# A two-layer decoder trunk on one core: the program's begin by contraction halves, its end shared among three engines, extra identity transposes, and one slab rounded earlier

## The chip, the core and the metric

The kernel runs on one core of a Trainium2 chip. The metric is the device time in microseconds of one execution; a trace of one profiled execution of the kernel before is read beside it.

## The reference, cut to what matters

Six sub-layers in a row work on x, 512 tokens by 1024 features, float32. After each stands a LayerNorm.

```python
def swiglu(x, w1, w3, w2):
    return (jax.nn.silu(x @ w1) * (x @ w3)) @ w2
# DEPTH = 2, D_FF = 2816; w = 1/2 for the gated (SwiGLU) layers, 1 for the mixers
for l in range(DEPTH):
    x = layer_norm(ALPHA * x + 0.5 * swiglu(x, w1[l,0], w3[l,0], w2[l,0]), ...)
    h = hybrid_attention(x, ...) if l % 2 == 0 else hgrn2(x, ...)
    x = layer_norm(ALPHA * x + h, ...)
    x = layer_norm(ALPHA * x + 0.5 * swiglu(x, w1[l,1], w3[l,1], w2[l,1]), ...)
```

## The kernel before, in words

The program has six phases, called n = 0 to 5: gated layer, attention, gated layer, gated layer, HGRN, gated layer. Every large product is made of three passes in a rounded float32 format: each operand is split into a high part (a rounded copy) and a low part (the operand minus its high part), and TensorE adds high x high, high x low and low x high (`three`, L1388 to L1390).

**Weights.** They come in slabs of 128 x 2048 numbers, 1 MB each, into a ring of three buffers `raw`; SP issues the loads in order (`load_slab`, L514). ScalarE makes the high part of a whole slab (`high`, L726, into `w_hi`), GpSimd the low part in four quarters of 128 x 512 (`low`, L664, into `w_lo`); for the first two slabs of the program VectorE makes the low part instead (`first_low`, L1258). Semaphores `hi_ready` and `lo_ready` count slabs. A slab buffer can be rounded into again when TensorE has finished its last user.

**Activations.** x stays in SBUF as four tiles of 128 tokens. At a phase's begin TensorE turns each tile with eight identity transposes (L1409) into two PSUM banks, four contraction blocks of 128 features in each bank; ScalarE copies a bank as high part into `xt_hi` (L731), VectorE makes the low part in `xt_lo` (L950). `begin` on TensorE turns tiles 0 and 1, waits for the first slab and the low parts, runs the first products for the first 256 tokens (two blocks of outputs from the first slab, one from the second), turns tiles 2 and 3, and goes on. Where the phase before is a gated layer (n = 1, 3, 4), tiles 0 and 1 are turned inside that layer's last products instead.

**A gated layer** projects 256 columns at a time with w1 and w3 (`up`), and works the down projection two groups at a time by a scheme with seven products of half size (P1 to P7) instead of eight. For it VectorE makes sums of operands (`left_sum`, L973; `right_sum`, L989) and low parts (L979, L995), ScalarE high parts (L750, L759). The four pairs are p = 0 to 3. In pair 0, TensorE runs `up` of slab s0+4, P1, P2, then `up` of slab s0+5. ScalarE's order for pair 0 is: high parts of A12, S1, B11, then `high(s0 + 5)`, then S2, S3, S4, A22. Every engine works its own queue strictly in the written order, and waits on semaphores in it.

**The end of a phase** (`last_down_and_norm`): the last down projection gives eight pieces of 512 features, in order of tile and half. VectorE adds the two pieces of a tile to x (`add_piece`, L1051), takes moments (L1211 to L1215), GpSimd makes rstd (L671), and `normalise` is two VectorE operations of 128 x 1024 with a wait for rstd between: centre and multiply by the gain `lng` (L1222), then scale by rstd and add the bias `lnb` (L1226). In the last phase SP stores a tile when `ln_done` counts it (L611).

**The program's begin**, in the kernel before: SP loads x tile 0, slab 0, x tile 1, slab 1, x tiles 2 and 3, three small inputs. ScalarE's order is: turned tile 0, slab 0, turned tile 1, slab 1, turned tiles 2 and 3. VectorE follows the same order with the low parts.

Of the kernel before, what the change touches and what calls it, by code (L numbers as in the profile page):

```python
# [25 lines left out]
F32 = mybir.dt.float32  # L26
F32R = mybir.dt.float32r
ALU = mybir.AluOpType
# [172 lines left out]
def build_trunk(nc, x_in, w1, w3, w2, ln_g, ln_b, aw_in, sinks, aw_out, hw_in, hnorm, hw_out, lbs_in, out,  # L201
# [23 lines left out]
    with ExitStack() as ctx:  # L225
# [109 lines left out]


        x_loaded = [sem(f"x_loaded{t}") for t in range(NT)]
        ident_zeroed = sem("ident_zeroed")
        consts_ready = sem("consts_ready")
        raw_landed = [sem(f"raw_landed{i}") for i in range(RING)]  # L340
# [24 lines left out]
        var_ready = sem("var_ready")  # L365
        rstd_ready = sem("rstd_ready")
        centred = sem("centred")
        ln_done = sem("ln_done")
        turn_done = sem("turn_done")
        xt_hi_done = sem("xt_hi_done")  # L370
# [137 lines left out]
        def _(sp):  # L508
# [36 lines left out]
            def load_x(t):  # L545
                sp.dma_start(x[:, t, :], x_in[0, t * P:(t + 1) * P, :]).then_inc(x_loaded[t], 16)

            def load_small():
# [4 lines left out]
            load_x(0)  # L553
            for n, (kind, wi, _, _) in enumerate(phases):
                s0 = bases[n][0]
                if kind == "ffn":
                    l, f = wi
                    a, b, c = w1[l, f], w3[l, f], w2[l, f]
                    load_slab(s0, up_slab(a, 0))
                    if n == 0:  # L560
                        load_x(1)
                    load_slab(s0 + 1, up_slab(b, 0))
                    if n == 0:
                        load_x(2)
# [23 lines left out]
                else:  # L588
                    for s, (name, g) in enumerate(mixer_slabs(kind)):
                        if s == RING:  # L590
                            load_params(n)
                        if kind == "attn":
                            swa, moba = 8 * HD, 8 * HD + 4 * HD
                            col = {"q": g * GW if g < 2 else moba + (g - 2) * GW, "kv": swa,
                                   "kb": moba + 512 + (g - 2) * GW, "vb": moba + 1024 + (g - 2) * GW}
                            src = down_slab(aw_out[0], g) if name == "down" else \
                                aw_in[0][:, col[name]:col[name] + GW].rearrange("(c p) n -> p c n", p=P)
                        else:
                            src = down_slab(hw_out[0], g) if name == "down" else \
# [3 lines left out]
                        if n == 0 and s == 0:  # L603
                            load_x(1)
                        if n == 0 and s == 1:
                            load_x(2)
                            load_x(3)
                            load_small()
            for t in range(NT):
                sp.wait_ge(ln_done, NT * last_phase + t + 1)  # L610
                sp.dma_start(out[0, t * P:(t + 1) * P, :], x[:, t, :]).then_inc(out_stored, 16)  # L611
            sp.wait_ge(out_stored, 16 * NT)


        @block.gpsimd
        def _(pool):
# [55 lines left out]
                                       ALU.pow).then_inc(rstd_ready, 1)  # L672


            pool.wait_ge(lo_ready, 2)
            low(2)
            for n, (kind, _, _, _) in enumerate(phases):
                s0 = bases[n][0]
                if kind == "ffn":
# [3 lines left out]
                    for j, tiles in enumerate(((0, 1), (2, 3), ())):  # L683
                        if n < last_phase:
                            if j == 2:
                                pool.wait_ge(ln_done, NT * (n + 1))
                            low(s0 + FFN_RING + j)
                        norm_powers(n, tiles)
                else:
                    slabs, plan = mixer_slabs(kind), mixer_schedule(kind)  # L690
                    if kind == "attn":
# [29 lines left out]
        def _(act):  # L721
# [50 lines left out]
                turn_high(turn, 2)  # L772
                turn_high(turn, 3)

            turn_high(0, 0)
            high(0)
            turn_high(0, 1)
            high(1)
            turn_high(0, 2)
            turn_high(0, 3)  # L780
# [74 lines left out]
            for n, (kind, _, _, _) in enumerate(phases):  # L855
                s0, K0, H0 = bases[n]
                if kind == "ffn":
# [7 lines left out]
                    gates(G0 + 1)  # L865
                    right_high(n, fi, 0, "B21")
                    for p in range(NP):
                        left_high(fi, p, "A12")
                        left_high(fi, p, "S1")
                        right_high(n, fi, p, "B11")  # L870
                        high(s0 + 4 * p + 5)
                        for name in ("S2", "S3", "S4", "A22"):
                            left_high(fi, p, name)
                        gates(G0 + 2 * p + 2)
# [64 lines left out]
                                high(s0 + s)  # L939
                if n < last_phase:  # L940
                    turn_all_high(n + 1, bases[n + 1][0] + 2)


        @block.vector
        def _(dve):
# [257 lines left out]
            def last_down_and_norm(n, K, weight):  # L1203
# [28 lines left out]

                add_pieces(0)
# [25 lines left out]
            turn_low(0, 0)  # L1261
            first_low(0)
            turn_low(0, 1)
            first_low(1)
            turn_low(0, 2)
            turn_low(0, 3)
# [118 lines left out]
        def _(pe):  # L1385
# [6 lines left out]
            def features(out_, slot, j, tok):  # L1392

                for c in range(DC):
                    cols = slice(c * GW + j * P, c * GW + (j + 1) * P)
# [24 lines left out]
            def product(n, f, p, name, b0):  # L1420
# [7 lines left out]
                for t in range(2):  # L1428
# [6 lines left out]
                                   (b_hi_[:, c, :], b_lo_[:, c, :]), c == 0, c == 1)  # L1435
                    mm.then_inc(product_done, 1)

            def begin(n, first_two):

                K = bases[n][1]
                if n == 0 or phases[n - 1][0] != "ffn":
                    turn(n, 0)
                    turn(n, 1)
                pe.wait_ge(lo_ready, bases[n][0] + 1)
                if n:
                    pe.wait_ge(y_added, FREE_AT_START + 8 * K - 2)
                pe.wait_ge(xt_lo_done, 8 * n + 4)
# [101 lines left out]
            def ffn_first_two(s0):  # L1551
                def first_two(s, half, tiles):
                    tok = slice(half * T // 2, (half + 1) * T // 2)
                    for j in tiles:
                        mm = features(bank[2 * s + j][:, tok], slot_of[s0 + s], j, tok)
# [238 lines left out]
```

## Time and profile before

| what | value |
| --- | --- |
| median of 3 runs | 2015.11 us (2015.10 to 2016.25) |
| the profiled execution | 2015.4 us, its span 2013.7 us |
| TensorE products | busy 1970.4 us, 98% of the span |
| VectorE | 1064.2 us, 53% |
| GpSimd | 921.8 us, 46% |
| ScalarE | 629.7 us, 31% |
| mean granted TensorE clock | 0.993 of full |

The span goes from the first to the last instruction. PE is TensorE (PEld its weight loads), DVE VectorE, ACT ScalarE, POOL GpSimd, SP the engine that issues the loads (SPq its queue). L1388 is line 1388 of the kernel before. A busy engine can be blocked inside an instruction: the time then stands in that instruction's duration. Idle time of an engine that is not on the path to the end costs nothing.

### The profile page before, as it was taken

The page shows a single profiled execution, that of the slowest core. Times are in us where ns is not written, and L with a number is a line of the kernel's source. Part 1 is how long each engine was busy: PE and PEld are TensorE (multiplying, and loading weights), DVE is VectorE, ACT ScalarE, POOL GpSimd, SP SyncE. Part 2 cuts the span into 40 slices and gives each one's busy share as a digit, 9 for nine tenths or more (in the row PEclk, how much of TensorE's full clock was granted, in tenths as well). Part 3 has the DMA queues.
Part 4 walks back from the last instruction along what each step waited for, and adds up shares of the span by engine and source line. Part 5 has one row for each costly group of instructions (what it writes and reads, how often), then busy time and mean ns, then how long its engine had stood idle before and what let it go on. Part 6 is the DMA issues. An engine that isn't in the chain of part 4 may idle for free.

```text
span 2013.7 us, 25063 instructions
## 1 busy us (share of the span) xinstructions
PE 1970.4 (98%) x10329; PEld 1682.5 (84%) x10329; DVE 1064.2 (53%) x1467; ACT 629.7 (31%) x786; POOL 921.8 (46%) x598
## 2 busy tenths in 40 slices
PE   8999999999989999999999999999999999999997
PEld 7888888988879888888988888898998988888886
DVE  2555472554363665654466656353543674466545
ACT  3333232254332333322233332232232123233330
POOL 4554464632223655445456535543443344465533
PEclk9999999999999999999999999999999999999999
DMA  6232323221204233232423323241211203323221
GB/s 231 84 107 82 126 84 105 89 84 43 68 16 147 84 111 109 74 105 84 147 84 105 104 85 105 84 126 59 68 64 64 63 25 123 126 84 120 89 85 42
DMA packets 135137, 185.45 MB, mean 92 GB/s; under 512 B 3168, under 2 KB 119024, under 8 KB 135024
## 3 DMA queue, kind: packets, MB, share of 16 engines
q1 hardware_dynamic: 134864, 183.59, 27.4%
q8 instruction: 82, 1.34, 0.3%
q10 hardware_dynamic: 160, 0.26, 0.1%
q14 instruction: 31, 0.25, 0.0%
HBM read 181.48 MB, written 2.10 MB: 91 GB/s over the span
## 4 chain that ended last, share of the span: by engine, by line
PE 92%; DVE 4%; POOL 3%; ACT 1%; issue 0%; DMA 0%; SPq 0%; DVEq 0%; ACTq 0%
PE psum L1388 28%; PE psum L1389 28%; PE psum L1390 28%; PE psum L1651 3%; POOL w_lo L664 2%; PE psum L1627 1%; PE psum L1594 1%; PE psum L1409 1%; PE psum L1609 1%; DVE x L1051 0%; ACT w_hi L726 0%; DVE x L1222 0%; PE psum L1689 0%; PE psum L1679 0%; DMA raw<-in_ffn_w 0%
## 5 line engine op out<-in xcount | busy, mean ns | idle before, releaser
L664 POOL TENSOR_TENSOR w_lo<-raw,w_hi 128x512 fp32r<-128x512 f32 x524 | 867.0, 1686 | 929.2 <-ACT w_hi L726 904.6
L1388 PE MATMUL psum<-xt_hi,w_hi 128*128 128x512 f32 (+1 forms) x1824 | 680.0, 373 | 11.9 <-DVE xt_lo L950 7.4
L1389 PE MATMUL psum<-xt_lo,w_hi 128*128 128x512 f32 (+1 forms) x1824 | 674.9, 370 | 0.0
L1390 PE MATMUL psum<-xt_hi,w_lo 128*128 128x512 f32 (+1 forms) x1824 | 674.9, 370 | 0.0
L1388 PEld LDWEIGHTS psum<-xt_hi,w_hi 128*128 128x128 f32 x1824 | 347.6, 191 | 75.5 <-issue 12.1
L1390 PEld LDWEIGHTS psum<-xt_hi,w_lo 128*128 128x128 f32 x1824 | 347.2, 190 | 57.4
L1389 PEld LDWEIGHTS psum<-xt_lo,w_hi 128*128 128x128 f32 x1824 | 347.7, 191 | 55.4
L726 ACT ACTIVATE w_hi<-raw 128x2048 fp32r<-128x2048 f32 x133 | 253.7, 1910 | 304.9 <-PE psum L1390 304.0
L1011 DVE SCALAR_TENSOR_TENSOR x<-psum,x 128x512 f32<-128x512 f32 x224 | 146.0, 685 | 134.8 <-PE psum L1390 131.1
L740 ACT ACTIVATE gate<-psum 128x512 f32<-128x512 f32 x88 | 52.5, 597 | 310.1 <-PE psum L1390 310.0
L1388 PE MATMUL psum<-w_hi,h_hi 128*128 128x512 f32 x352 | 140.1, 398 | 2.6 <-DVE x L1051 2.6
L1051 DVE SCALAR_TENSOR_TENSOR x<-psum,x 128x512 f32<-128x512 f32 x128 | 85.9, 687 | 105.4 <-PE psum L1390 105.1
L1388 PE MATMUL psum<-w_hi,xt_hi 128*128 128x256 f32 (+2 forms) x448 | 140.5, 314 | 0.0
L1389 PE MATMUL psum<-w_lo,h_hi 128*128 128x512 f32 x352 | 138.6, 394 | 0.0
L1390 PE MATMUL psum<-w_hi,xt_lo 128*128 128x256 f32 (+2 forms) x448 | 137.6, 307 | 0.0
L1389 PE MATMUL psum<-w_lo,xt_hi 128*128 128x256 f32 (+2 forms) x448 | 137.5, 307 | 0.0
L1390 PE MATMUL psum<-w_hi,h_lo 128*128 128x512 f32 x352 | 137.3, 390 | 0.0
L1389 PE MATMUL psum<-w_lo,a_hi 128*128 128x512 f32 x320 | 126.2, 394 | 0.0
L1388 PE MATMUL psum<-w_hi,a_hi 128*128 128x512 f32 x320 | 125.5, 392 | 0.0
L958 DVE TENSOR_TENSOR hid<-psum,gate 128x512 f32<-128x512 f32 x48 | 33.2, 692 | 173.7 <-PE psum L1390 173.7
L1390 PE MATMUL psum<-w_hi,a_lo 128*128 128x512 f32 x320 | 124.3, 389 | 0.0
L995 DVE TENSOR_TENSOR w_lo<-raw_odd,w_hi 128x1024 fp32r<-128x1024 f32 x48 | 59.1, 1232 | 110.5 <-ACT w_hi L759 110.5
(153 smaller groups left out, 2206.9 us busy)
## 6 DMA issues: line engine op xcount, KB each, us to landing
raw<-in_ffn_w SPq DMA_DIRECT2D x116, 1024.0 KB, 5.4
raw_odd<-in_ffn_w SPq DMA_DIRECT2D x16, 1024.0 KB, 5.0
raw<-in_hgrn_w_in SPq DMA_DIRECT2D x16, 1024.0 KB, 5.4
raw<-in_attn_w_in SPq DMA_DIRECT2D x9, 1024.0 KB, 5.3
raw<-in_attn_w_out SPq DMA_DIRECT2D x4, 1024.0 KB, 4.9
raw<-in_hgrn_w_out SPq DMA_DIRECT2D x4, 1024.0 KB, 4.9
lng<-in_ln_g SPq DMA_DIRECT2D x6, 512.0 KB, 4.2
lnb<-in_ln_b SPq DMA_DIRECT2D x6, 512.0 KB, 5.3
```

The costliest lines, as they stand in the source:

```text
L664: op = pool.tensor_tensor(w_lo[:, slot_of[s], cols], raw[:, slot_of[s], cols], w_hi[:, slot_of[s], cols].bitcast(F32), ALU.subtract)
L726: act.activation(w_hi[:, slot_of[s], :], raw[:, slot_of[s], :], ACT.Copy).then_inc(hi_ready, 1)
L740: act.activation(gate[:, j, :], bank[j][:], ACT.Silu).then_inc(gate_done, 1)
L958: dve.tensor_tensor(dst[:, j, :], bank[2 + j][:], gate[:, j, :], ALU.mult).then_inc(hid_done, 1)
L995: dve.tensor_tensor(lo, right_source(n, name), hi.bitcast(F32), ALU.subtract).then_inc(right_lo_ready, 1)
L1011: dve.scalar_tensor_tensor(out=x_piece(row, t, half), in0=bank[b0 + t][:], scalar=weight / ALPHA, in1=x_piece(row, t, half), op0=ALU.mult, ...
L1051: dve.scalar_tensor_tensor(out=part, in0=banks[k % len(banks)][:], scalar=weight / ALPHA, in1=part, op0=ALU.mult, op1=ALU.add).then_inc(y_ ...
L1388: pe.matmul(out_, w[0], xs[0], start=first, stop=False)
L1389: pe.matmul(out_, w[0], xs[1], start=False, stop=False)
L1390: return pe.matmul(out_, w[1], xs[0], start=False, stop=last)
L1409: mm = pe.transpose(bank[4 + 2 * (t % 2) + b][:, c * P:(c + 1) * P], x[:, t, (4 * b + c) * P:(4 * b + c + 1) * P], ident[:])
L1651: mm = pe.matmul(out_, ks[:, g % 2, h, chunk], rhs, start=True, stop=True)
```

## The change

It has four parts.

1. The program's first phase begins by contraction halves. x tiles 0 and 1 are loaded in halves of 512 features, slab 0 in two halves of four contraction blocks each; the order of the loads is x half 0 of tiles 0 and 1, slab half 0, x half 1 of both tiles, slab half 1, slab 1, then as before. TensorE turns block 0 of both tiles, then block 1 of both; ScalarE and VectorE round block, slab half, block, slab half. The first product group (first slab, first output block, first 256 tokens) starts when the first half is ready and waits for the second half ahead of its fifth contraction block. Behind the transposes of block 0 stand twelve extra identity transposes, behind those of block 1 eight, written to a bank that nobody reads.
2. At the begins of n = 2 and n = 5 (behind the mixers) fourteen extra identity transposes stand between the wait for the added pieces and the wait for `xt_lo`.
3. In pair 0 of every gated layer ScalarE rounds slab s0+5 ahead of A12, S1 and B11 instead of behind them.
4. At the end of the last phase VectorE centres tiles 0 and 1, ScalarE scales them by rstd, GpSimd adds the bias. VectorE goes on to tiles 2 and 3 and waits for tiles 0 and 1 to be finished ahead of normalising tile 2. The last operation on tile 3 is cut in two halves of 512 features, and each half is stored by itself.

In the diff `sp`, `pool`, `act`, `dve` and `pe` are the queues of SP, GpSimd, ScalarE, VectorE and TensorE.

```diff
+            for t in range(2):
+                load_x_half(t, 0, x_half_loaded[t])
...
-                    load_slab(s0, up_slab(a, 0))
                     if n == 0:
-                        load_x(1)
+                        load_first_half(0, up_slab(a, 0), raw_half_landed)
+                        for t in range(2):
+                            load_x_half(t, 1, x_loaded[t])
+                        load_first_half(1, up_slab(a, 0), raw_landed[0])
+                    else:
+                        load_slab(s0, up_slab(a, 0))
                     load_slab(s0 + 1, up_slab(b, 0))
...
+            for half in range(2):
+                cols = slice(half * HALF, (half + 1) * HALF)
+                sp.wait_ge(ln_done, NT * last_phase + NT + half)
+                sp.dma_start(out[0, (NT - 1) * P:T, cols], x[:, NT - 1, cols]).then_inc(out_stored, 16)
...
+            def shift(n, tiles):
+                pool.wait_ge(par_loaded[1], 16 * (n + 1))
+                for t in tiles:
+                    pool.wait_ge(scaled, t + 1)
+                    pool.tensor_tensor(x[:, t, :], x[:, t, :], lnb[:], ALU.add).then_inc(ln_done, 1)
...
+            first_turn_high(0)
+            act.wait_ge(raw_half_landed, 16)
+            act.activation(w_hi[:, 0, 0:SLAB // 2], raw[:, 0, 0:SLAB // 2], ACT.Copy).then_inc(hi_half_ready, 1)
+            first_turn_high(1)
+            act.wait_ge(raw_landed[0], 16)
+            act.activation(w_hi[:, 0, SLAB // 2:SLAB], raw[:, 0, SLAB // 2:SLAB], ACT.Copy).then_inc(hi_ready, 1)
...
                     for p in range(NP):
+                        if p == 0:
+                            high(s0 + 5)
                         left_high(fi, p, "A12")
                         left_high(fi, p, "S1")
                         right_high(n, fi, p, "B11")
-                        high(s0 + 4 * p + 5)
+                        if p:
+                            high(s0 + 4 * p + 5)
...
+            for t in range(2):
+                act.wait_ge(centred, NT * last_phase + t + 1)
+                act.wait_ge(rstd_ready, NT * last_phase + t + 1)
+                act.activation(x[:, t, :], x[:, t, :], ACT.Copy, scale=rstd[:, t:t + 1]).then_inc(scaled, 1)
...
+                if n == last_phase:
+                    dve.wait_ge(par_loaded[0], 16 * (n + 1))
+                    centre(0)
+                    centre(1)
+                    add_pieces(2)
+                    moments(2)
+                    add_pieces(3)
+                    moments(3)
+                    dve.wait_ge(ln_done, NT * n + 2)
+                    normalise(2)
+                    centre(3)
+                    dve.wait_ge(centred, NT * n + 4)
+                    normalise_halves(3)
+                    return
...
+            def keep_clock(times):
+                for _ in range(times):
+                    pe.transpose(bank[1][:, 0:P], ident[:], ident[:])
...
+                if n == 0:
+                    for b in range(2):
+                        for t in range(2):
+                            pe.wait_ge((x_half_loaded, x_loaded)[b][t], 16)
+                            for c in range(4):
+                                mm = pe.transpose(bank[4 + 2 * t + b][:, c * P:(c + 1) * P],
+                                                  x[:, t, (4 * b + c) * P:(4 * b + c + 1) * P], ident[:])
+                            mm.then_inc(turn_done, 1)
+                        keep_clock((12, 8)[b])
+                    pe.wait_ge(lo_half_ready, 1)
+                    pe.wait_ge(xt_lo_done, 2)
+                else:
...
                     pe.wait_ge(y_added, FREE_AT_START + 8 * K - 2)
+                    if phases[n - 1][0] != "ffn":
+                        keep_clock(14)
+                    pe.wait_ge(xt_lo_done, 8 * n + 4)
```

## Rows read from the trace of the kernel before

**Rows 1.** Waits of TensorE: us in total, times, longest us.

```profile
PE psum L1388 <- DVE xt_lo L950: 7.4, 3, 2.6
PE psum L1388 <- POOL w_lo L664: 4.2, 4, 1.1
```

**Rows 2.** Timeline of the begin: start, length, engine, operation, [idle before <- what ended it].

```profile
4.72 1.94 PE L1409 MATMUL psum<-ident,x 128*128 128x128 f32 x8 [4.72 <-DMA x<-in_x]
...
5.85 0.60 ACT L731 ACTIVATE xt_hi<-psum 128x512 fp32r<-128x512 f32 x1 [3.76 <-PE psum L1409]
...
7.88 1.91 ACT L726 ACTIVATE w_hi<-raw 128x2048 fp32r<-128x2048 f32 x1 [0.59 <-DMA raw<-in_ffn_w]
...
9.30 1.97 PE L1409 MATMUL psum<-ident,x 128*128 128x128 f32 x8 [2.63 <-DMA x<-in_x]
...
12.28 1.91 ACT L726 ACTIVATE w_hi<-raw 128x2048 fp32r<-128x2048 f32 x1 [0.38 <-DMA raw<-in_ffn_w]
...
13.46 0.55 PE L1388 MATMUL psum<-xt_hi,w_hi 128*128 128x256 f32 x1 [2.20 <-DVE xt_lo L950]
...
14.22 2.29 DVE L1258 TENSOR_TENSOR w_lo<-raw,w_hi 128x2048 fp32r<-128x2048 f32 x1 [0.90 <-ACT w_hi L726]
...
24.03 1.91 PE L1409 MATMUL psum<-ident,x 128*128 128x128 f32 x16
```

**Rows 3.** Stretches: length, busy (count) of PE, PEld, DVE, ACT, POOL, PEclk, DMA, GB/s.

```profile
13.40:17.40 4.00, 3.94 (x18) 3.97 (x19) 2.29 (x1) 0.79 (x1) 0.00 (x0) 1.00 0.49 162
17.40:24.00 6.60, 6.60 (x56) 6.60 (x55) 0.00 (x0) 0.00 (x0) 0.00 (x0) 1.00 1.05 376
604.70:608.00 3.30, 3.30 (x18) 3.30 (x17) 3.23 (x8) 0.00 (x0) 1.53 (x2) 0.51 0.00 0
1646.80:1652.40 5.60, 5.57 (x26) 5.60 (x27) 5.43 (x12) 0.00 (x0) 3.08 (x4) 0.50 0.00 0
1382.50:1389.40 6.90, 6.90 (x25) 6.07 (x26) 2.56 (x5) 0.00 (x0) 2.32 (x2) 0.54 0.47 150
```

**Rows 4.** Timeline of TensorE behind the attention phase, and in the HGRN phase.

```profile
598.39 1.03 PE L1409 MATMUL psum<-ident,x 128*128 128x128 f32 x8
600.68 1.09 PE L1409 MATMUL psum<-ident,x 128*128 128x128 f32 x8 [1.25 <-DVE x L1226]
604.36 0.35 PE L1388 MATMUL psum<-xt_hi,w_hi 128*128 128x256 f32 x1 [2.59 <-DVE xt_lo L950]
...
1382.47 1.94 PE L1651 MATMUL psum<-arena 128*128 128x64 f32 x10 [2.14 <-DVE arena L1156]
```

**Rows 5.** Timeline of VectorE at the same begin.

```profile
601.74 2.48 DVE L950 TENSOR_TENSOR xt_lo<-psum,xt_hi 128x512 fp32r<-128x512 f32 x4
```

**Rows 6.** Timeline of the second slab of the first gated layer, all engines.

```profile
62.56 0.69 DVE L958 TENSOR_TENSOR hid_odd<-psum,gate 128x512 f32<-128x512 f32 x1 [4.75 <-PE psum L1390]
...
65.50 1.90 ACT L726 ACTIVATE w_hi<-raw 128x2048 fp32r<-128x2048 f32 x1
...
67.48 7.62 POOL L664 TENSOR_TENSOR w_lo<-raw,w_hi 128x512 fp32r<-128x512 f32 x1 [17.01 <-ACT w_hi L726]
...
72.73 1.22 DVE L989 TENSOR_TENSOR raw<-right_sums,raw 128x1024 f32<-128x1024 f32 x1
74.08 2.10 DVE L989 TENSOR_TENSOR raw_odd<-raw_odd,raw 128x1024 f32<-128x1024 f32 x1
...
78.57 1.27 POOL L664 TENSOR_TENSOR w_lo<-raw,w_hi 128x512 fp32r<-128x512 f32 x1
...
79.89 0.51 PE L1388 MATMUL psum<-xt_hi,w_hi 128*128 128x512 f32 x1 [1.06 <-POOL w_lo L664]
```

**Rows 7.** The end: timeline of VectorE, and the stores (KB each, us to landing).

```profile
1999.63 1.51 DVE L1051 SCALAR_TENSOR_TENSOR x<-psum,x 128x512 f32<-128x512 f32 x2
...
2009.34 1.28 DVE L1226 SCALAR_TENSOR_TENSOR x<-x,rstd,lnb 128x1024 f32<-128x1024 f32 x1
...
out_x<-x SPq DMA_DIRECT2D x4, 512.0 KB, 2.6
```

More of the change, by code:

```diff
@@ L337, in build_trunk @@
         x_loaded = [sem(f"x_loaded{t}") for t in range(NT)]
+        x_half_loaded = [sem(f"x_half_loaded{t}") for t in range(2)]
+        raw_half_landed = sem("raw_half_landed")
+        hi_half_ready = sem("hi_half_ready")
+        lo_half_ready = sem("lo_half_ready")
         ident_zeroed = sem("ident_zeroed")
@@ L367, in build_trunk @@
         centred = sem("centred")
+        scaled = sem("scaled")
         ln_done = sem("ln_done")
@@ L602, in _ @@
                         load_slab(s0 + s, src)
[L603 to L609, printed above, removed]
+            for t in range(NT - 1):
                 sp.wait_ge(ln_done, NT * last_phase + t + 1)
                 sp.dma_start(out[0, t * P:(t + 1) * P, :], x[:, t, :]).then_inc(out_stored, 16)
-            sp.wait_ge(out_stored, 16 * NT)
+            for half in range(2):
+                cols = slice(half * HALF, (half + 1) * HALF)
+                sp.wait_ge(ln_done, NT * last_phase + NT + half)
+                sp.dma_start(out[0, (NT - 1) * P:T, cols], x[:, NT - 1, cols]).then_inc(out_stored, 16)
+            sp.wait_ge(out_stored, 16 * (NT + 1))
         @block.gpsimd
@@ L688, in _ @@
                         norm_powers(n, tiles)
+                        if n == last_phase and j == 0:
+                            shift(n, tiles)
                 else:
@@ L1231, in low_, with centre, normalise_halves @@
                         turn_low(n + 1, t)
+                def centre(t):
+                    dve.scalar_tensor_tensor(out=x[:, t, :], in0=x[:, t, :], scalar=meanvar[:, t, 0:1],
+                                             in1=lng[:], op0=ALU.subtract, op1=ALU.mult).then_inc(centred, 1)
+                def normalise_halves(t):
+                    dve.wait_ge(rstd_ready, NT * n + t + 1)
+                    for half in range(2):
+                        cols = slice(half * HALF, (half + 1) * HALF)
+                        dve.scalar_tensor_tensor(out=x[:, t, cols], in0=x[:, t, cols], scalar=rstd[:, t:t + 1],
+                                                 in1=lnb[:, cols], op0=ALU.mult, op1=ALU.add).then_inc(ln_done, 1)
                 add_pieces(0)
@@ L1259, in first_low, with first_turn_low, first_low_half @@
                                   ALU.subtract).then_inc(lo_ready, 1)
-            turn_low(0, 0)
-            first_low(0)
-            turn_low(0, 1)
+            def first_turn_low(b):
+                for t in range(2):
+                    dve.wait_ge(xt_hi_done, 2 * b + t + 1)
+                    part = (slice(None), slice(4 * b, 4 * b + 4), slice(t * P, (t + 1) * P))
+                    dve.tensor_tensor(xt_lo[part], bank[4 + 2 * t + b].rearrange("p (c n) -> p c n", n=P),
+                                      xt_hi[part].bitcast(F32), ALU.subtract).then_inc(xt_lo_done, 1)
+            def first_low_half(half, ready, done):
+                dve.wait_ge(ready, 1)
+                cols = slice(half * SLAB // 2, (half + 1) * SLAB // 2)
+                dve.tensor_tensor(w_lo[:, 0, cols], raw[:, 0, cols], w_hi[:, 0, cols].bitcast(F32),
+                                  ALU.subtract).then_inc(done, 1)
+            first_turn_low(0)
+            first_low_half(0, hi_half_ready, lo_half_ready)
+            first_turn_low(1)
+            first_low_half(1, hi_ready, lo_ready)
             first_low(1)
@@ L1390, in three, with features @@
                 return pe.matmul(out_, w[1], xs[0], start=False, stop=last)
-            def features(out_, slot, j, tok):
+            def features(out_, slot, j, tok, first_slab=False):
                 for c in range(DC):
+                    if first_slab and c == DC // 2:
+                        pe.wait_ge(lo_ready, 1)
+                        pe.wait_ge(xt_lo_done, 4)
                     cols = slice(c * GW + j * P, c * GW + (j + 1) * P)
@@ L1554, in first_two @@
                     for j in tiles:
-                        mm = features(bank[2 * s + j][:, tok], slot_of[s0 + s], j, tok)
+                        mm = features(bank[2 * s + j][:, tok], slot_of[s0 + s], j, tok,
+                                      s0 + s + half + j == 0)
                         if half:
```

26 lines of the change are left out of this document (16 added, 10 removed).

## The prediction, made before the changed kernel was run

> **What bounds the kernel now.** I read the page first, then the waits of TensorE, then its timeline at every place where it waits, with ScalarE, VectorE and GpSimd beside it. TensorE is busy for 1970.4 of the span's 2013.7 us, so the time is TensorE's queue plus what stands before its first product, in its gaps, in stretches at half clock, and behind its last product. The waits [rows 1] name two kinds of gap that the edits touch: 7.4 us behind DVE xt_lo (three begins of a phase) and 4.2 us behind POOL w_lo, four times 1.06. The third is the loads of x, 4.72 and 2.63 us [rows 2]. The granted clock [rows 3] is 0.51 for 3.3 us after the begin at 604.7 and 0.50 for 5.6 us after the one at 1646.8. In the kernel's first 4.0 us of products the row says 1.00, yet only 18 matmuls fit, against 56 in the next 6.6 us (118 ns each): that is half pace, 1.2 instead of 2.4 GHz. What stands there at half pace could be had in half the time: 2.0, 1.6 and 2.8 us.
>
> **Part 1, the first phase's begin.** Before, the landings are [rows 2] 4.72 (x tile 0, 0.5 MB), 7.88 (first slab, 1.5 MB in all), 9.30 (x tile 1, 2 MB) and 12.28 (second slab, 3 MB): about 3.0 us per MB. The new order by that rate: x halves 4.0 and 4.7, first half slab 6.3, the other x halves 7.0 and 7.8, second half slab 9.3, second slab 12.3 as before. It adds three DMA issues on SP ahead of the second slab; the data of the six ahead of it last until 9.3, so SP has more than a microsecond for each, and I count nothing for them.
> Transposes: 8 take 1.94 at half pace, so the first eight run from 4.0 to 5.9 and twelve more at 0.21 us until 8.4, past the 7.8 at which the x halves are there; the second eight end at 10.3, the last eight extra ones at 12.0. ScalarE takes 0.60 for a turned block and half of 1.91 for a half slab: high of half 0 is done at 7.6, its low part (half of VectorE's 2.29) at 8.9, so TensorE, not data, sets the first product: 12.0. The second half: last block copied at 11.0, half slab at 12.0, its low part at 13.3. Before, the first product of all started at 13.46. Before the transposes of tiles 2 and 3 stand 72 products (two blocks of the first slab and one of the second, 24 each). 12 are done when the second half becomes ready at 13.3, and 60 follow at 0.118 to 0.12: until 20.6, where before it was 24.03. I take 3.4 us. The second slab (ScalarE 12.3 to 14.2, VectorE to 16.5) is wanted after 36 products, at 17.7. Bounds: if the clock rises already during the extra transposes, these shrink and the whole chain moves to 19.4, 4.6 us; if it rises only after 4 us of products, as before, TensorE starts at 12.0, does 19 in 4.0 us and 53 in 6.3, ending at 22.3: 1.7 us. So this part is -1.7 to -4.6.
>
> **Part 2, fourteen extra transposes at the begins behind the two mixers.** The last tile of the mixer is turned at 600.68 to 601.77, the residual pieces are added about then, and VectorE's four low parts (2.48 us from 601.74) release the products at 604.36 [rows 4, 5], and then the products run. Fourteen at full pace (1.09 - 0.27 over 7, 0.117 each) take 1.7 us and end at 603.5, 0.9 us before the release: they cost nothing. At half pace they would take 3.1 and cost 0.5 each time. What they can give is the stretches at half clock, 1.6 + 2.8 = 4.4 us. Do transposes hold the clock? Between 598.39 and 604.36 TensorE ran nothing but 16 transposes (2.1 of 6.0 us) [rows 4], and the first product at 604.36 was still quick; yet in the HGRN stage a gap of 2.14 us alone, at 1380.3, brought the clock down to 0.54 for 6.9 us [rows 3, 4]. So transposes seem to count. With fourteen more, TensorE stands still for 1.25 and 0.9 us instead of 1.25 and 2.6. Over the 1.25 before 600.68 the clock stayed up: the eight transposes behind it took 1.09, not 1.94. I take all 4.4; bounds +1.0 and -4.4.
> The Trainium skill says otherwise ("TensorE: Matmul & The Clock Gate", Part 4: PE-mode transpose): transposes do not count as busy for the clock the way products do. By that rule part 2 gives nothing and part 1 its 1.7; it is the first rival.
>
> **Part 3, the gated layers' second slab.** In each of the four gated layers TensorE waits 1.06 us for the low part of slab s0+5 [rows 1, 6]. ScalarE rounds it at 65.50; the edit puts this before the copy of A12, which starts when VectorE's product at 62.56 is done, so the rounding can start when TensorE has finished the slot's last user, at 62.56 too, and ends at 64.5, 3 us earlier. The copies behind it come 1.1 us later at first (A12 done at 65.0; VectorE's chain comes to it at 65.1) and are level again after B11; nothing waits. But GpSimd's first quarter of that slab took 7.62 us, from 67.48 to 75.1, where others take 1.27: it got through only in the 0.13 us pause that VectorE makes before the sum at 74.08, which in turn took 2.10 instead of 1.22 [rows 6]. From 63.29 until 73.95 VectorE runs 14 operations with two inputs in SBUF end to end, the one at 72.73 the last. GpSimd asking at 64.6 instead of 67.5 meets the same queue: its first quarter still ends at 75.1, the second behind that sum at 77.3, the last two 1.27 later each, at 79.84, and TensorE waits 1.06 as before. Should VectorE pause at 65.1, a quarter gets in there, but then the sum at 74.08 comes 1.15 later and the last quarter ends at the same time. I take 0; the other bound is the whole wait, 4 x 1.06 = 4.2 us.
>
> **Part 4, the end.** VectorE now leaves two scalings to ScalarE and two additions to GpSimd, 2 x 1.28 us of its queue. But it needed them in a pause: its pair of additions for tile 2 begins at 1999.63 and takes 1.51 us [rows 7], so the second piece, 0.69 long, began at 2000.45, when TensorE had it: some 0.2 us of pause are left even with all four scalings and additions in VectorE's queue. From there its queue is the same instructions: tile 2's and 3's moments and normalisation until 2010.6 [rows 7]. The new wait, on tiles 0 and 1 being shifted, stands before tile 2's normalisation at 2005.5: centring done at 1997.1, ScalarE some 1.1 us each, GpSimd two quarters' length each, 2.5 us [rows 6], from 1997.0, so 2002.0; even with a second operation three times as long it is in time. Behind that wait are only VectorE's last operations. What is left is the store of the last tile in halves: 512 KB land in 2.6 us [rows 7], moving about half of that time, so the second half lands about 0.6 us earlier. I take 0.6; bounds 0 and -0.9.
>
> **Sum.** 3.4 + 4.4 + 0 + 0.6 = 8.4 us. The profiled execution's 2015.4 (span 2013.7 and 1.7 around it) becomes 2007.0; it stood 0.3 above the median of 2015.11, so the median becomes **2006.7**. A shift of some us moves later gaps (the HGRN stage's at 1380 costs 3 us of clock) against whatever the clock counts in; I allow 1.5 either way.
>
> **Rivals.**
> (a) The extra transposes do not count for the clock. For: sixteen transposes from 598.39 on did not keep it beyond 604.7. Against: it lasted 6 us, longer than over the gap at 1380. Then 1.7 + 0.6: 2012.8.
> (b) GpSimd's earlier start pays: it finds a hole before VectorE's chain closes, four quarters get in. For: it asks 3 us earlier. Against: no boundary between VectorE's operations let it in for 6.5 us, in all four layers. Then 4.2 more: 2002.5.
> (c) Slower: the halved loads. Six requests where three were, rows half as long; if they land at 4 instead of 3 us per MB, the second half slab comes at 11.5 and its low part at about 15.5, and TensorE, idle from 13.4, drops to half pace for 4 us: 60 products end at 24.7, +0.7. With (a)'s failure to hold the clock elsewhere and fourteen transposes at half pace twice (+1.0), the second slab (16 + 4.2 us until low, wanted at 20) adding 0.3 and the end giving nothing, it is +2.0: 2017.1. It decides from a landing of the second half slab later than about 11. Against: the slab's own 1 KB rows already move at the full rate.
> (d) The begin of phase 0 works half as well and one of two clock stretches stays: about -5, 2010.
>
> **How the numbers follow.** Forecast 0.50, (a) 0.17, (b) 0.19, (c) 0.03, (d) 0.11. A change within 0.2% (4.0 us) cannot be told from none here. The forecast, (b) and (d) are faster than that: 0.80, less a little for (d), 0.78; (a) and most of (c) are the same, 0.20; slower by over 0.2%, 0.02. The range runs from 2001.8 (b with luck) to 2011.3, leaving out (a) and (c).
>
> **What would show it.** Start: transposes of tiles 2 and 3 at 20.6 instead of 24.03, a first product near 12 or earlier with a pause before the fifth contraction block. Clock: no stretch near 0.5 behind the two mixers. Second slab: ScalarE's rounding at 62.6 relative to the old clock of the layer, GpSimd's first quarter then about 10.5 us long, TensorE's wait still 1.06; if the wait is gone, part 3 is wrong. End: VectorE idle until the piece that was at 2000.45, and the same 10.2 us from there to its last operation. If the gain is below 4 us, the clock part is wrong; if above 11, part 3.

## The result, and the profile after

The changed kernel takes **1999.68 us** in the median of 4 runs (1997.73 to 2000.55) against 2015.11: ratio **0.9922**, 95% interval 0.9908 to 0.9936. The forecast was 2006.7 with a range from 2001.8 to 2011.3; it is 7.0 us too slow and the range does not hold the time. The profiled execution took 1998.96 us, its span is 1997.2 (before 2013.7): 16.5 us less, where the sum had 8.4.

Putting the two kernels' products side by side, in order and without the extra transposes, shows where TensorE runs ahead of its old timeline. A place's gain is what it adds to the lead; behind the mixers it grows over the products that ran at half pace before:

| where | start before | start after | gained here, us | forecast |
| --- | --- | --- | --- | --- |
| turns of tiles 2 and 3 in the begin | 24.03 | 20.78 | 3.2 | 3.4 |
| the four second slabs (near 80, 670, 1025, 1713) | 79.89 | 75.41 | 1.34 each, 5.4 | 0 |
| begin of n = 2 and of n = 5 | 604.36, 1646.83 | 599.61, 1634.71 | 1.55 + 2.63 = 4.2 | 4.4 |
| the HGRN phase | 1382 | 1374 | 3.2 | within +-1.5 |
| last product's start to the end of the span | 10.92 long | 10.45 long | 0.5 | 0.6 |

The five are 16.5 us. They are those of one execution, the second fastest of the four; between the medians lie 15.4 us. Now the views that show them, all of the kernel after. First the waits of TensorE (line waited on and by, us in total, times, longest):

```profile
PE psum L1539 <- DMA x<-in_x: 4.1, 1, 4.1
...
PE psum L1471 <- DVE xt_lo L994: 1.2, 2, 0.6
```

Against [rows 1], `xt_lo` fell from 7.4 us in three waits to 1.2 in two, and there is no row for POOL w_lo at all. The timeline of TensorE in the begin (start, length, operation, idle before and what ended it):

```profile
4.13 1.94 PE L1539 MATMUL psum<-ident,x 128*128 128x128 f32 x8 [4.13 <-DMA x<-in_x]
5.87 2.53 PE L1527 MATMUL psum<-ident 128*128 128x128 f32 x12
8.23 1.28 PE L1539 MATMUL psum<-ident,x 128*128 128x128 f32 x8
9.35 1.04 PE L1527 MATMUL psum<-ident 128*128 128x128 f32 x8
10.14 0.36 PE L1471 MATMUL psum<-xt_hi,w_hi 128*128 128x256 f32 x1
...
12.89 0.39 PE L1471 MATMUL psum<-xt_hi,w_hi 128*128 128x256 f32 x1 [1.08 <-DVE w_lo L1340]
...
17.81 0.39 PE L1471 MATMUL psum<-xt_hi,w_hi 128*128 128x256 f32 x1 [0.34 <-DVE w_lo L1327]
...
20.78 1.91 PE L1495 MATMUL psum<-ident,x 128*128 128x128 f32 x16
```

Eight transposes took 1.94 us first and 1.04 last: half pace, then full pace, with nothing but transposes between. The products start at 10.14, at full pace; against [rows 2] the first product stood at 13.46. Then data sets the pace, twice: the second half slab's low part, and the second slab's. ScalarE's timeline says why the last is late:

```profile
10.52 1.06 ACT L814 ACTIVATE w_hi<-raw 128x1024 fp32r<-128x1024 f32 x1 [0.37 <-DMA raw<-in_ffn_w]
13.51 1.92 ACT L753 ACTIVATE w_hi<-raw 128x2048 fp32r<-128x2048 f32 x1 [1.93 <-DMA raw<-in_ffn_w]
```

The second slab landed 1.2 us later than before (13.51 against 12.28), in a load order with three more requests ahead of it, though with the same bytes. In the seven traces with this order its rounding starts at 12.80 to 13.62 us, in the six with the old one at 11.95 to 12.28.

The second slab of the first gated layer, VectorE, ScalarE and GpSimd (rows of three timelines):

```profile
59.30 1.92 ACT L753 ACTIVATE w_hi<-raw 128x2048 fp32r<-128x2048 f32 x1 [9.39 <-PE psum L1473]
61.24 0.68 DVE L1017 TENSOR_TENSOR hid<-left_sum,hid 128x512 f32<-128x512 f32 x1
61.30 6.90 POOL L682 TENSOR_TENSOR w_lo<-raw,w_hi 128x512 fp32r<-128x512 f32 x4 [14.05 <-ACT w_hi L753]
61.84 1.79 DVE L1023 TENSOR_TENSOR h_lo<-hid_odd,h_hi 128x512 fp32r<-128x512 f32 x1
63.56 1.78 DVE L1017 TENSOR_TENSOR hid_odd<-hid_odd,hid 128x512 f32<-128x512 f32 x1
65.27 1.78 DVE L1023 TENSOR_TENSOR a_lo<-left_sum,a_hi 128x512 fp32r<-128x512 f32 x1
66.97 2.31 DVE L1039 TENSOR_TENSOR w_lo<-raw,w_hi 128x1024 fp32r<-128x1024 f32 x1
```

In [rows 6] one quarter took 7.62 us because GpSimd stood blocked; here all four take 6.90. The two engines take turns: each of VectorE's four operations beside them is 1.1 us longer than its kind (1.79 for 0.68, 2.31 for 1.22), each quarter about 1.75.

The begin of n = 2, TensorE, and stretches with the granted clock (columns as in [rows 3]):

```profile
596.02 1.09 PE L1495 MATMUL psum<-ident,x 128*128 128x128 f32 x8 [1.26 <-DVE x L1270]
597.31 1.72 PE L1527 MATMUL psum<-ident 128*128 128x128 f32 x14 [0.20 <-DVE x L1095]
599.61 0.39 PE L1471 MATMUL psum<-xt_hi,w_hi 128*128 128x256 f32 x1 [0.58 <-DVE xt_lo L994]
```

```profile
595.00:615.00 20.00, 18.20 (x151) 17.76 (x152) 16.30 (x25) 6.69 (x9) 12.12 (x10) 1.00 0.25 75
1373.50:1388.50 15.00, 14.96 (x86) 13.06 (x87) 6.66 (x13) 3.92 (x6) 2.40 (x2) 1.00 0.23 72
1503.00:1506.40 3.40, 3.40 (x18) 3.40 (x18) 1.84 (x5) 0.00 (x0) 1.17 (x1) 0.51 0.24 46
1630.00:1660.00 30.00, 28.09 (x232) 27.61 (x233) 17.25 (x27) 8.67 (x13) 15.65 (x13) 1.00 0.49 172
```

The half-clock stretches behind both mixers are gone, and so is the one near 1380, though its gap is still there:

```profile
1373.54 2.00 PE L1756 MATMUL psum<-arena 128*128 128x64 f32 x16 [2.12 <-DVE arena L1200]
```

2.12 us of standstill against 2.14 in [rows 4], and no fall behind it this time. Left is 3.4 us near 1503 at 0.51 (before it was near 1516).

The end, VectorE, ScalarE and GpSimd:

```profile
1979.88 2.35 ACT L985 ACTIVATE x<-x,rstd 128x1024 f32<-128x1024 f32 x2 [12.63 <-DVE x L1280]
1981.17 4.76 POOL L698 TENSOR_TENSOR x<-x,lnb 128x1024 f32<-128x1024 f32 x2 [0.92 <-ACT x L985]
1983.09 0.69 DVE L1095 SCALAR_TENSOR_TENSOR x<-psum,x 128x512 f32<-128x512 f32 x1 [2.05 <-PE psum L1473]
...
1993.33 1.42 DVE L1287 SCALAR_TENSOR_TENSOR x<-x,rstd,lnb 128x512 f32<-128x512 f32 x2
```

VectorE now stands idle for 2.05 us before tile 2's first piece and 0.67 before its second.

### The profile page after: what moved, and what is told of

It reads as the page before. It is cut to its first block, busy times and chain, and to the rows that moved or that the text cites. A ratio compares the mean times of both kernels' runs of the same rounds, so it can differ in the third digit from the quotient of the medians.

```text
span 1997.2 us, 25169 instructions
## 1 busy us (share of the span) xinstructions
PE 1966.2 (98%) x10377; PEld 1679.2 (84%) x10377; DVE 1082.1 (54%) x1467; ACT 632.0 (32%) x789; POOL 909.7 (46%) x600
## 3 DMA queue, kind: packets, MB, share of 16 engines
q8 instruction: 82, 1.34, 0.3%
## 4 chain that ended last, share of the span: by engine, by line
PE 95%; DVE 3%; DMA 0%; ACT 0%; issue 0%; SPq 0%; POOL 0%; DVEq 0%
PE psum L1471 29%; PE psum L1472 29%; PE psum L1473 29%; PE psum L1756 3%; PE psum L1732 1%; PE psum L1699 1%; PE psum L1495 1%; PE psum L1714 1%; DVE x L1095 0%; DMA raw<-in_ffn_w 0%; PE psum L1794 0%; PE psum L1784 0%; DVE x L1266 0%; PE psum L1787 0%; PE psum L1774 0%
## 5 line engine op out<-in xcount | busy, mean ns | idle before, releaser
L682 POOL TENSOR_TENSOR w_lo<-raw,w_hi 128x512 fp32r<-128x512 f32 x524 | 850.1, 1654 | 929.8 <-ACT w_hi L753 905.2
L1471 PEld LDWEIGHTS psum<-xt_hi,w_hi 128*128 128x128 f32 x1824 | 343.8, 188 | 64.8 <-issue 4.0
```

The source lines that it names most:

```text
L682: op = pool.tensor_tensor(w_lo[:, slot_of[s], cols], raw[:, slot_of[s], cols], w_hi[:, slot_of[s], cols].bitcast(F32), ALU.subtract)
L1471: pe.matmul(out_, w[0], xs[0], start=first, stop=False)
```

## The experiments

Each is timed against the kernel before on the same chip; the ratio is to that, with its 95% interval.

**1. Part 3 alone** (`order_only`): in the kernel before, as in the change,

```diff
                     for p in range(NP):
+                        if p == 0:
+                            high(s0 + 5)
                         left_high(fi, p, "A12")
...
-                        high(s0 + 4 * p + 5)
+                        if p:
+                            high(s0 + 4 * p + 5)
```

> The kernel before with part 3 alone (slab s0+5 rounded ahead of A12 in pair 0). Theory: asked early, just as VectorE reaches A12 at the moment its high part is finished, GpSimd gets the port and the two take turns (quarters about 1.75 us, VectorE's operations beside them about 1.8), the four waits of TensorE of 1.06 us vanish, each worth about 1.3 us with the restart: span 2013.7 - 5.3 = 2008.4, median near 2009.8. Rival (my prediction's part 3: the port is closed until VectorE pauses before its last sum): first quarter about 10.5 us long, four waits of 1.06 remain, 2015.1. A second rival, that the wait vanishes only because the clock held at other places: the waits would stay here.

Measured: 2010.64 us, ratio 0.9978 (0.9969 to 0.9988). The four waits on POOL w_lo are gone. Its rows, GpSimd and VectorE:

```profile
64.61 0.68 DVE L976 TENSOR_TENSOR hid<-left_sum,hid 128x512 f32<-128x512 f32 x1
64.66 6.90 POOL L664 TENSOR_TENSOR w_lo<-raw,w_hi 128x512 fp32r<-128x512 f32 x4 [14.08 <-ACT w_hi L726]
65.21 1.79 DVE L982 TENSOR_TENSOR h_lo<-hid_odd,h_hi 128x512 fp32r<-128x512 f32 x1
```

So part 3 gives the whole wait by itself; nothing of part 1 or 2 is needed for it. It is no accident of one trace either: in the six traces with the new order (with the later experiments) all 24 of these requests got in at the next boundary, in the five with the old order and no pause all 20 were blocked for 7.62 us. The median gained 4.3, not 5.4. By the products' starts in the two traces, 0.9 us was lost where the half-clock stretch near 602 became twice as long (6.8 us for 3.4; part of it falls into TensorE's wait) and 0.1 in the begin.

**2. One pause in VectorE's chain, the order untouched** (`pause_only`):

```diff
                         right_low(n, fi, p, "B11")
+                        if p == 0:
+                            then(dve.memset(stats[:, 0, 0:1], 0.0))
```

`then` makes VectorE wait for its own operation.

> The kernel before with one tiny VectorE operation (a memset of one column of stats, awaited by VectorE itself) in pair 0 between the low part of B11 and that of S2, which opens a pause of about 0.1 us in VectorE's chain just after GpSimd has asked for its first quarter. Nothing is rounded earlier. Theory: any pause lets GpSimd in, and once in it takes turns with VectorE: first quarter about 1.8 instead of 7.62 us, all four done by about 75 on the old clock, no wait of 1.06 us in the gated layers, 2009.8. Rival (what counts is asking 3 us earlier): the wait stays, 2015.1 or up to 1 us more for the pause.

Measured: 2010.11 us, ratio 0.9974 (0.9965 to 0.9983); no wait on w_lo.

```profile
67.78 6.90 POOL L664 TENSOR_TENSOR w_lo<-raw,w_hi 128x512 fp32r<-128x512 f32 x4 [17.01 <-ACT w_hi L726]
68.37 0.06 DVE L1306 MEMSET stats<- 128x1 f32 x1
68.48 3.35 DVE L979 TENSOR_TENSOR a_lo<-hid,a_hi 128x512 fp32r<-128x512 f32 x2
```

GpSimd asks at the old moment (67.78, against 67.48 with products that run 0.3 us later) and still has its four quarters in 6.90 us. It is the lock-out that cost the wait, not the late start; and once GpSimd is in, it keeps getting its turn without further pauses.

**3. The same request, later** (`ask_late`): in pair 0 `high(s0 + 5)` stands behind A22.

```diff
-                        high(s0 + 4 * p + 5)
+                        if p:
+                            high(s0 + 4 * p + 5)
                         for name in ("S2", "S3", "S4", "A22"):
                             left_high(fi, p, name)
+                        if p == 0:
+                            high(s0 + 5)
```

> The kernel before, and in the first pair alone high(s0 + 5) comes after A22 instead of ahead of A12, so GpSimd asks for the second slab's rounding near 69.5 us, about 2 us later than before (67.48), while VectorE is in its 512-column sums and not in the 1024-column sum of B11. Theory (the first operand VectorE is in when GpSimd asks decides whether GpSimd waits for one instruction or for the whole row of them): the first quarter takes about 1.8 us, the four are done near 77.4, the four waits of 1.06 on w_lo are gone, median about 2010 as in order_only. Rival (it is the earlier start that pays, 64.6 against 67.5): a later start makes the waits no smaller, four waits of 1 us or more stay, median 2015 or more.

Measured: 2015.36 us, ratio 1.0004 (0.9994 to 1.0013). The theory falls. The group of GpSimd's w_lo from 68 to 82 us (count, shortest/median/longest ns, first and last start), and TensorE behind it:

```profile
L664 POOL TENSOR_TENSOR w_lo<-raw,w_hi x6: 1257/2266/5534, 69.2 to 81.7; 128x512 fp32r<-128x512 f32 x6
```

```profile
79.52 0.50 PE L1391 MATMUL psum<-xt_hi,w_hi 128*128 128x512 f32 x1 [1.04 <-POOL w_lo L664]
```

Asked inside a 512-column operation (68.89), the first quarter was still blocked, for 5.53 us, until the pause at 73.7. Which operand VectorE is in does not decide.

**4. Slack ahead of the copies** (`order_slack`): experiment 1, and three tiny awaited operations on VectorE ahead of the sum S1 of pair 0. It asks whether GpSimd gets in only because VectorE comes just in time for ScalarE's delayed high part of A12.

```diff
                         hiddens(G0 + 2 * p + 1)
+                        if p == 0:
+                            for _ in range(3):
+                                then(dve.memset(stats[:, 0, 0:1], 0.0))
```

> order_only with three tiny awaited VectorE operations ahead of the first sum of pair 0, so that VectorE's chain starts some 0.35 us later and the high part of A12 is there well before VectorE comes to it; GpSimd still asks about 3 us earlier than in the kernel before. Theory (in order_only GpSimd got in because VectorE had to wait some hundredths of a us for A12's high part, which opened its chain): no pause, so the port stays closed, first quarter about 9 us long, the waits of TensorE back, about 1.4 us each with the shift: 2015 to 2017. Rival (asking early is what counts, the chain of 512-column operations lets GpSimd in by itself): quarters of 1.8 us as in order_only, no waits, 2010.6.

Measured: 2009.55 us, ratio 0.9970 (0.9958 to 0.9981); the waits stay gone.

```profile
64.23 0.69 DVE L976 TENSOR_TENSOR hid<-hid 128x512 f32<-128x512 f32 x1
64.61 6.56 POOL L664 TENSOR_TENSOR w_lo<-raw,w_hi 128x512 fp32r<-128x512 f32 x4 [14.08 <-ACT w_hi L726]
64.83 1.78 DVE L976 TENSOR_TENSOR hid<-left_sum,hid 128x512 f32<-128x512 f32 x1
```

GpSimd got in one operation sooner, ahead of the sum S2, which needs nothing of ScalarE's. So the gain doesn't hang on the copies coming just in time either. What lets it in at 64.8 but not at 68.1 or 69.5 stays open.

It is not the operation at which it asks. In pair 2 of the first gated layer, which no edit touches, GpSimd asks 0.03 us ahead of VectorE's next operation in the kernel before, and is shut out; in `order_only` it asks at the same boundary, 0.05 us ahead, and is let in (the kernel before, then `order_only`):

```profile
192.34 8.23 POOL L664 TENSOR_TENSOR w_lo<-raw,w_hi 128x512 fp32r<-128x512 f32 x1 [13.56 <-ACT w_hi L726]
192.37 1.22 DVE L995 TENSOR_TENSOR w_lo<-raw,w_hi 128x1024 fp32r<-128x1024 f32 x1
...
191.04 1.29 POOL L664 TENSOR_TENSOR w_lo<-raw,w_hi 128x512 fp32r<-128x512 f32 x1 [13.56 <-ACT w_hi L726]
191.09 2.33 DVE L998 TENSOR_TENSOR w_lo<-raw,w_hi 128x1024 fp32r<-128x1024 f32 x1
```

So a few hundredths of a microsecond can separate the two outcomes; no run shows by what rule. And the change does not end the lock-outs: in the kernel after twelve first quarters, those of pairs 1 to 3 in each gated layer, still take 8.1 us. No wait of TensorE hangs on them.

**5. The change without part 3** (`no_order`): the edit of experiment 1 undone in the kernel after.

> The kernel after without its part 3 (the gated layers' second slab is rounded in the old order). If the parts add, the second slab's four waits come back at 1.06 to 1.34 us each: 1999.7 + 5.4 = 2005.1 us, four rows of L1756 or L1471 with about 1.06 us on w_lo. Rival: the earlier begin shifts GpSimd's request to another of VectorE's instructions and the waits are gone without the order: 1999.7.

Measured: 2005.62 us, ratio 0.9956 (0.9941 to 0.9971). TensorE's waits:

```profile
PE psum L1468 <- POOL w_lo L682: 4.2, 4, 1.1
```

All four are back. Its span is 2004.0, 6.8 above the kernel after: 4 x 1.34, and 1.4 mostly from clock stretches. It has one of 6.8 us near 1380, which costs it 3.2, where the kernel after has one of 3.4 near 1503, which costs 1.6:

```profile
1378.40:1385.20 6.80, 6.80 (x22) 5.70 (x22) 2.01 (x4) 0.00 (x0) 1.40 (x2) 0.50 0.47 154
```

**6. Part 2 alone** (`keep14_only`): in the kernel before, with the helper `keep_clock` of the change,

```diff
                     pe.wait_ge(y_added, FREE_AT_START + 8 * K - 2)
+                if n and phases[n - 1][0] != "ffn":
+                    keep_clock(14)
                 pe.wait_ge(xt_lo_done, 8 * n + 4)
```

> The kernel before with part 2 alone (fourteen extra transposes at the begins behind the mixers). Theory: the two stretches at half clock behind the mixers (3.3 and 5.6 us) vanish: 4.2 us, less or more by what the HGRN stage's gaps then cost: 2010.9, between 2008 and 2012.5. Rival (transposes do not count as busy): both stretches stay, 2015.1.

Measured: 2009.27 us, ratio 0.9975 (0.9966 to 0.9985). Stretches:

```profile
600.00:610.00 10.00, 9.13 (x74) 8.69 (x75) 9.83 (x19) 2.89 (x3) 7.08 (x6) 1.00 0.01 2
1382.00:1385.40 3.40, 3.40 (x11) 2.74 (x10) 2.01 (x4) 0.00 (x0) 0.70 (x1) 0.50 0.41 115
...
1640.00:1652.00 12.00, 11.22 (x94) 10.78 (x93) 11.79 (x19) 2.89 (x3) 6.55 (x6) 1.00 0.01 1
```

With fourteen transposes the clock stays up behind both mixers, and by the products' starts TensorE gains 1.55 us at the first and 2.6 at the second. The other 2.1 us of this trace are not part 2's: the stretch near 1382 has halved (1.6 us), though the nearest edit ahead of it is 780 us away, and the first loads landed sooner (0.6).

**7. Part 1 alone** (`begin_only`), **and the same without its twenty extra transposes** (`begin_no_extra`, `keep_clock((12, 8)[b])` left out).

> The kernel before with part 1 alone (the first phase begun by halves, with the 12 and 8 extra transposes). Theory: 3.2 us earlier at the transposes of tiles 2 and 3, nothing else touched directly: 2011.9, give or take 3 us of HGRN and mixer clock stretches that move against the clock's own rhythm. Rival (no such rhythm, the HGRN saving of 3.1 us in the changed kernel had another cause): 2011.9 with the granted clock below 1 in the same four places as before.

> begin_only without its 12 and 8 extra transposes. Theory (the extra transposes bring the clock up before the first product): the x halves turn earlier (from 7.0 instead of 8.2), but the products start at half pace for 3 to 4 us; transposes of tiles 2 and 3 at about 22, 1.2 us later than with the extras. Rival (transposes do not count for the clock; the halves alone gave the gain): 20.8 or earlier, as with the extras.

Measured: 2011.59 us, ratio 0.9983 (0.9974 to 0.9993), and 2010.48 us, ratio 0.9978 (0.9969 to 0.9988). TensorE of the second:

```profile
7.57 1.97 PE L1512 MATMUL psum<-ident,x 128*128 128x128 f32 x8 [1.63 <-DMA x<-in_x]
9.19 0.56 PE L1444 MATMUL psum<-xt_hi,w_hi 128*128 128x256 f32 x1
...
12.44 0.39 PE L1444 MATMUL psum<-xt_hi,w_hi 128*128 128x256 f32 x1 [0.54 <-DVE w_lo L1313]
...
20.08 1.91 PE L1468 MATMUL psum<-ident,x 128*128 128x128 f32 x16
```

Without them the products begin 0.9 us sooner, the first ten at half pace, and TensorE waits for the same half slab all the same; the turns of tiles 2 and 3 come at 20.08, not at the 22 expected, and with them at 20.58 (`begin_only`) and 20.78 (the kernel after). The medians don't measure the begin alone: in the kernel before the half-clock stretches at n = 2, near 1383, near 1516 and at n = 5 are 3.4, 6.8, 3.4 and 6.8 us long, in `begin_only`, where nothing behind the first 20 us was edited, 6.8, 3.4, 6.8 and 3.4.

**8. The end without ScalarE and GpSimd** (`end_halves`): the kernel after, VectorE normalising tiles 0 and 1 by itself, ScalarE's and GpSimd's operations on them left out.

```diff
                 if n == last_phase:
-                    dve.wait_ge(par_loaded[0], 16 * (n + 1))
-                    centre(0)
-                    centre(1)
+                    normalise(0)
+                    normalise(1)
...
-                    dve.wait_ge(ln_done, NT * n + 2)
```

> The changed kernel with VectorE doing all of the scaling and bias of tiles 0 and 1 itself; the last tile's last operation and its store stay in halves. Theory (part 4's offload fills a pause, only the half store counts): from the start of the last product to the end of the span 10.5 us as in the changed kernel (11.0 before), median as the changed kernel's, 1999.7 +- 1.5. Rival (the offload is what shortens the end): 11.0 us, 0.5 us slower.

Measured: 2000.38 us (1997.19 to 2001.38), ratio 0.9924 (0.9909 to 0.9938), no different from the change; from the last product's start to the end of its span 10.5 us, as with the two engines' help.

```profile
1980.68 1.29 DVE L1264 SCALAR_TENSOR_TENSOR x<-x,rstd,lnb 128x1024 f32<-128x1024 f32 x1
1981.88 1.51 DVE L1089 SCALAR_TENSOR_TENSOR x<-psum,x 128x512 f32<-128x512 f32 x2
```

**9. Transposes ahead of two HGRN levels** (`keep_hgrn`), **and that without the begin's extras** (`hgrn_no_start`: `keep_clock(0)` there).

```diff
                 else:
+                    if (g, a) in ((0, 6), (2, 3)):
+                        pe.wait_ge(level_merged, 7 * g + a - 2)
+                        for _ in range(14 if g == 0 else 9):
+                            pe.transpose(bank[2 + a % 2][:, 0:P], ident[:], ident[:])
                     pe.wait_ge(level_kept, 8 * g + a)
```

> The changed kernel with 14 and 9 more extra transposes in the two gaps of the HGRN stage (ahead of level 6 of group 0, 2.12 us, and level 3 of group 2, 1.38 us), into the bank that the level's own products overwrite. Theory (the HGRN saving of 3.1 us in the changed kernel was the clock not falling at the first gap, by chance of where the gap lay against the clock's rhythm): no stretch at half clock between the begin and the end in any run, executions close together at 1997.5, instead of 1997.7 to 2000.6. Rival (the fall comes from the 128x64 products and not from the gap): falls remain, 1999.7.

> keep_hgrn (the kernel after with 14 and 9 identity transposes more ahead of the HGRN levels (0,6) and (2,3)) without the 12 and 8 transposes that the begin issues. If the transposes of the begin cost what begin_no_extra showed (turns of tiles 2 and 3 at 20.08 instead of 20.8), the median is about 0.7 us under keep_hgrn's 1997.6: 1996.9, with no stretch at half the clock behind the begin. Rival: they are what keeps the clock where the first mixer begins, and without them the clock's stretches fall elsewhere, 1998 to 2001.

Measured: 1997.61 us (1997.28 to 1998.63), ratio 0.9914 (0.9897 to 0.9931), and **1997.27 us** (1997.06 to 1997.58), ratio 0.9913 (0.9898 to 0.9928). Of `keep_hgrn`:

```profile
1370.62 1.69 PE L1749 MATMUL psum<-ident 128*128 128x128 f32 x14
1372.92 2.00 PE L1760 MATMUL psum<-arena 128*128 128x64 f32 x16 [0.61 <-DVE arena L1200]
```

```profile
1495.00:1525.00 30.00, 29.61 (x222) 28.00 (x221) 16.98 (x24) 8.05 (x9) 13.64 (x9) 1.00 0.19 58
```

No stretch at half clock is left between the begin and the end. One trace does not prove the fill, though: that of `end_halves`, with neither gap filled, has none either. The runs speak for it: all eight with the gaps filled lie between 1997.06 and 1998.63, while two of the kernel after's four and three of `end_halves`' four are above 2000. The second version's turns of tiles 2 and 3 came at 20.88, not at 20.1: its second x half landed late (turned at 7.86), and `keep_hgrn` with the extras had 20.10. So the turns' start varies by 0.8 us between executions, the extras show no gain or loss beyond that, and experiment 7's difference can't be put down to them. The two versions are not told apart; against the kernel after they are 2 us faster by medians taken on different chips, with intervals that overlap.

## Why the prediction was wrong

**Part 3 is the step that failed**, in the sentence "GpSimd asking at 64.6 instead of 67.5 meets the same queue: its first quarter still ends at 75.1". The term was put at 0 and measured 5.4 us. Rival (b), with 0.19, had the direction right and 4.2 us as its size; the hole it looked for was not needed. The step rested on [rows 6], where no boundary between VectorE's operations let GpSimd in. That is true of the boundaries behind 67.48, but it was taken for a rule of all of them. GpSimd asked at 64.66 in `order_only` and was in at the next boundary; the wait went alone with the order (experiment 1), came back without it (experiment 5), and went with the order untouched where VectorE paused (experiment 2). The price was also 5.4, not 4.2: TensorE gains 1.34 at each, the 1.06 of the wait's row and 0.28 around it.

**The second term is the clock in the HGRN phase**: 3.2 us gained in the profiled execution where 1.5 either way was allowed. The forecast had named that gap as worth about 3 us and shifting against the clock, and then did not carry the 3 into the bound. Experiments 1, 6 and 7 show such shifts without an edit nearby: a stretch twice as long in one place, half as long in another. That they follow from where the gap falls in time fits all runs; no run sets that time on purpose.

**Part 1**: 3.2 measured, 3.4 forecast, but by another way than its working, so the close sum is luck. The transposes at full pace came sooner (products from 10.14, not 12.0), as in the lower bound, which would have given 4.6; but the second half slab (TensorE waits 1.08) and the second slab (0.34) took that back. Both landed about 1.2 us later than the working had them: 10.5 for 9.3, and 13.5 for 12.3. It had said "I count nothing" for the three additional requests; no run separates them from the new order of the loads. The extra transposes, with which the working began, show no gain (experiments 7 and 9).

**Part 2**: 4.2 measured, 4.4 forecast. TensorE stood for 1.26, 0.20 and 0.58 us, and the fourteen took 1.72 in the shadow of the low parts. Rival (a) falls with the begin's rows (nothing but transposes ran while their pace rose) and with experiment 6. The page "TensorE: Matmul & The Clock Gate" of the Trainium skill, Part 4: PE-mode transpose, on which it leant, does not hold for these float32 identity transposes.

**Part 4**: 0.5 measured, 0.6 forecast, and the reason held: VectorE has 2.05 us of idle time where the two engines help, and without them still reaches tile 2's pieces in time (experiment 8). That leaves the halved last tile as what gives it; no run has the halves alone.

**Rival (c)** had a late second half slab, deciding from a landing at about 11. The high part started at 10.52, so the landing was half a microsecond short of that, and TensorE lost 1.08 us there. The rival's low part "at about 15.5" for a landing at 11.5 was mis-summed: in the trace the low part was done 2.3 us after the landing, which would give 13.8.

## What to carry to other kernels

An engine's lock-out seen at one moment is not a rule for an earlier one: when a request moves, the bound is the whole wait, and a 0.1 us pause in the blocking engine's chain is the cheap test and the cheap cure. Where a fall of the clock behind one gap costs some us, any edit ahead of it can change that cost; fill the gap itself, and the spread shrinks too (2.8 us between the fastest and slowest run of the change, 1.4 and 0.5 in the two versions of experiment 9, four runs each).

## What the hardware showed that I had not expected

- VectorE and GpSimd, both with two inputs in SBUF, either take turns or shut one out. With turns: four quarters in 6.90 us, VectorE's operations 1.1 us longer each. Shut out: 8.23 and 7.62 us [rows 6] and 5.53 us (`ask_late`) for one quarter of 1.27. The Trainium skill ("SBUF — State Buffer", Who interferes with whom) has a VectorE operation with two SBUF inputs contend with a GpSimd one that reads SBUF, and says of the shared ports: "Whoever issues first gets the shared pair for the whole instruction; the other fully blocks". The traces agree that there is contention, but show a block over five to nine of VectorE's operations, not over one. Which of the two comes is open: neither the width of VectorE's operation nor the just-in-time copies decide, and the same boundary gave both. A pause of about 0.1 us ended the block each time.
- The half-clock stretch near 1380 was 6.8, 3.4 or 0 us long behind the same gap of 2.1 us, by what had shifted hundreds of us before.
